# Small fp32 products on the two halves of TensorE in turn, in a four-layer hybrid network

## What is computed

```python
oa = gated_delta_rule(qa, ka, va, g.transpose(0, 2, 1), beta.transpose(0, 2, 1))
ob = moba_attention(split_heads(qb), split_heads(kb), split_heads(vb))
hc = mlstm_chunkwise(split_heads(qc), split_heads(kc), split_heads(v_c), i_pre, logf)
return jnp.concatenate([oa, ob, hc], axis=-1) @ w_out
```

```python
diff = bt[:, :, :, None, :] - bt[:, :, None, :, :]
dec = jnp.where(mask, jnp.exp(jnp.where(mask, diff, 0.0)), 0.0)
attn = jnp.einsum('bhtk,bhtsk->bhts', qt, dec * kt[:, :, None, :, :])
o_intra = jnp.einsum('bhts,bhsv->bhtv', attn, vt)
state = jnp.exp(b_last[:, :, 0, :])[..., None] * state + jnp.einsum(
    'bhsk,bhsv->bhkv', kt * jnp.exp(b_last - bt), vt)
```

## Time and profile before

| | |
|---|---|
| median of 3 runs | 2211.3 us (2209.76 to 2214.19) |
| the profiled execution | 2211.54 us |
| its span, first to last instruction | 2209.6 us |
| mean granted TensorE clock | 0.965 of full speed |
| busy: PE, PEld, DVE, ACT, POOL | 2058.1, 1914.5, 1644.6, 1082.2, 322.7 us |
| weight stream on the SP queue (q1) | 384.85 MB, 46.5% of 16 DMA engines' span |

### The profile page before, as it was taken

How to read it: one execution, slowest core, us unless ns; L and a number is a source line. 1 busy time by engine, 2 the same in 40 slices (tenths; PEclk the granted TensorE clock), 3 DMA queues, 4 the chain that set the end, 5 groups by cost and what they waited for, 6 DMA issues and landing times.

```text
span 2209.6 us, 35479 instructions
## 1 busy us (share of the span) xinstructions
PE 2058.1 (93%) x14804; PEld 1914.5 (87%) x14804; DVE 1644.6 (74%) x2175; ACT 1082.2 (49%) x1540; POOL 322.7 (15%) x269
## 2 busy tenths in 40 slices
PE   7999899999998999899989997898899988989998
PEld 7999789978987998799969986897799778968986
DVE  6698788566987578787575668986788588757884
ACT  4543473445434443553444434655565365646652
POOL 0200023010020002303010023520000136000020
PEclk9999999999999999899989998999999989999999
DMA  9888552134976578442225662332354532324442
GB/s 376 327 345 320 202 203 96 45 128 163 350 290 245 210 269 312 152 163 77 96 100 200 241 242 106 135 131 99 134 189 176 208 128 107 141 105 153 175 180 103
DMA packets 60079, 409.97 MB, mean 186 GB/s; under 512 B 6864, under 2 KB 6864, under 8 KB 13456
## 3 DMA queue, kind: packets, MB, share of 16 engines
q1 hardware_dynamic: 53712, 384.85, 46.5%
q0 software_dynamic: 5920, 22.43, 3.0%
q10 hardware_dynamic: 288, 0.42, 0.1%
HBM read 404.53 MB, written 3.15 MB: 185 GB/s over the span
## 4 chain that ended last, share of the span: by engine, by line
PE 74%; DVE 16%; ACT 4%; issue 2%; POOL 2%; DMA 1%; SPq 0%; POOLq 0%; DVEq 0%; ACTq 0%
PE ps L696 14%; PE ps L697 13%; PE ps L698 13%; PE ps L724 6%; PE ps L726 6%; PE ps L725 6%; DVE l L592 4%; PE ps L1755 2%; PE ps L709 2%; PE ps L710 2%; PE ps L711 2%; ACT h L577 1%; PE ps L1737 1%; PE ps L1632 1%; DMA w<-in_stream 1%
## 5 line engine op out<-in xcount | busy, mean ns | idle before, releaser
L696 PE MATMUL ps<-xh,h 128*128 128x256 f32 x2688 | 774.8, 288 | 30.7 <-DVE xl L913 8.7
L592 DVE TENSOR_TENSOR l<-w,h 128x2048 fp32r<-128x2048 f32 (+1 forms) x295 | 684.2, 2324 | 138.4 <-ACT h L577 137.9
L697 PE MATMUL ps<-xl,h 128*128 128x256 f32 x2688 | 762.6, 284 | 0.0
L698 PE MATMUL ps<-xh,l 128*128 128x256 f32 x2688 | 761.9, 283 | 0.0
L577 ACT CAST h<-w 128x2048 fp32r<-128x2048 f32 (+1 forms) x295 | 556.8, 1894 | 317.8 <-PE ps L726 145.3
L696 PEld LDWEIGHTS ps<-xh,h 128*128 128x128 f32 x2688 | 517.8, 193 | 43.8 <-issue 25.2
L697 PEld LDWEIGHTS ps<-xl,h 128*128 128x128 f32 x2688 | 517.7, 193 | 1.5 <-issue 1.4
L698 PEld LDWEIGHTS ps<-xh,l 128*128 128x128 f32 x2688 | 517.3, 192 | 0.0
L724 PE MATMUL ps<-h,hh 128*128 128x512 f32 x528 | 209.7, 397 | 9.0 <-DVE l L592 9.0
L726 PE MATMUL ps<-h,hl 128*128 128x512 f32 x528 | 207.5, 393 | 0.0
L725 PE MATMUL ps<-l,hh 128*128 128x512 f32 x528 | 207.3, 393 | 0.0
(11 more groups left out here) (413 smaller groups left out, 3030.0 us busy)
## 6 DMA issues: line engine op xcount, KB each, us to landing
w<-in_stream SPq DMA_DIRECT2D x361, 1024.0 KB, 4.9
GB<-in_vec POOLq DMA_DIRECT2D x20, 512.0 KB, 6.1
w<-in_stream SPq DMA_DIRECT2D x8, 512.0 KB, 4.1
gate<-in_vec POOLq DMA_DIRECT2D x6, 512.0 KB, 3.9
cst<-in_cst POOLq DMA_DIRECT2D x1, 1160.0 KB, 9.0
memf<-in_memT SPq DMA_DIRECT2D x2, 512.0 KB, 5.4
xf<-in_xT POOLq DMA_DIRECT2D x1, 1024.0 KB, 8.7
kv<-mk POOLq DMA_DIRECT2D x2, 512.0 KB, 6.3
```

Source lines behind the costliest of these rows:

```text
L592: e.tensor_tensor(k.L[m % NH][:, 0:z], k.W[n % NW][:, 0:z], k.H[m % NH][:, 0:z], SUB).then_inc(k.lo_done, 1)
L696: p.matmul(P[:, 0:T], H[:, r, o], xh[:, r, :], start=r == 0, stop=False)
L697: p.matmul(P[:, 0:T], H[:, r, o], xl[:, r, :], start=False, stop=False)
L698: i = p.matmul(P[:, 0:T], L[:, r, o], xh[:, r, :], start=False, stop=r == 7)
```

## The change

Every small product that uses half of the array's rows or gives half of its outputs is issued in turn with one of the other half. For that gdn's matrices of levels 0 to 5 are kept as their two diagonal blocks of 64x64, one in partitions 0 to 63 and one in 64 to 127 (`small`, 12 units of 64 columns), six units to a bank; a level has then two groups where it had four, on PE, DVE, ACT and POOL. The off-diagonal block goes to `AO`, and the inverse is written at last to the full `XF`, whose left half POOL clears once. The numbering of units changes (`unit`, `block`), so that a group for one half of the rows is followed by one for the other. `RB` is kept in partitions 64 to 127 too. hgrn's `A` holds only blocks of 64x64, one bank a level in turn instead of two. The constants shrink from 2320 to 1616 columns.

```diff
+def pe_halves(p, P, sem, left, right):
+
+    for j in range(6):
+        for r in (LO, HI):
+            x = p.matmul(P[r, j * 64:j * 64 + 64], left(r, j), right(r, j), start=True, stop=True)
+            if j == 5:
+                x.then_inc(sem, 1)
...
-    for lv in range(1, 7):
-        for g in range(4):
+    for lv in range(1, 6):
+        for g in range(2):
             b = GBANK[f"U{lv}", g]
             P = take(k, p, b)
...
+            pe_halves(p, P, s, lambda r, j: k.Al[r, 6 * g + j, :], lambda r, j: k.Xb[r, 6 * g + j, :])
             k.freed[b] = ga(l, f"U{lv}", g)
...
+                l_, r_ = (k.Ub, k.XT) if x else (k.XT, k.Ub)
+                pe_halves(p, P, s, lambda r, j: l_[r, 6 * g + j, :], lambda r, j: r_[r, 6 * g + j, :])
```

Decays and scores, by halves of the rows, into two banks:

```diff
+        for j in range(3):
+            for i, r in enumerate((LO, HI)):
+                g = 2 * n + i
+                h, a = unit(3 * g + j) if n < 2 else (OFF[3 * i + j], 1)
+                c = 64 * i + 32 * q + h
+                row = k.ident[r, c:c + 1].to_broadcast([64, 128])
+                x = p.matmul(P[i][:, j * 128:j * 128 + 128], row, k.RB[r, a * 128:a * 128 + 128], start=True, stop=True)
...
+            x = p.matmul(P[i][:, j * 128:j * 128 + 128], lT[r, pr, s * 128:s * 128 + 128], rT[r, pr, t * 128:t * 128 + 128], start=True, stop=True)
```

DVE, ACT and POOL in gdn:

```diff
-    v.tensor_copy(k.RB[Q0, :], G[Q0, ALL]).then_inc(s, 1)
+    for q in (Q0, Q2):
+        v.tensor_copy(k.RB[q, :], G[Q0, ALL]).then_inc(s, 1)
...
+        if g < 4:
+            v.tensor_tensor(k.AT[LO, u, :], P[LO, :, 0:64], k.Dk[LO, u, 0:64], MUL).then_inc(s, 1)
+            v.tensor_tensor(k.AT[HI, u, :], P[HI, :, 64:128], k.Dk[HI, u, 64:128], MUL).then_inc(s, 1)
+            v.tensor_tensor(k.AO[LO, u, :], P[LO, :, 64:128], k.Dk[LO, u, 64:128], MUL).then_inc(s, 1)
...
+            v.tensor_tensor(k.Xb[:, u, :], k.Xb[:, u, :], P, SUB).then_inc(s, 1)
...
+                e.copy(k.Ub[:, u, :], P).then_inc(s, 1)
...
+            g_.tensor_tensor(k.Al[:, 6 * g:6 * g + 6, :], k.AT[:, 6 * g:6 * g + 6, :], m, MUL).then_inc(k.gg.sem, 1)
```

hgrn's levels, states and sums:

```diff
+    P = take(k, p, 4 + n % 2)
+    for j in range(8):
+        for o, r in enumerate((LO, HI)):
+            c = slice(j % 2 * 128 + o * 64, j % 2 * 128 + o * 64 + 64)
+            i = p.matmul(P[r, j * 64:j * 64 + 64], Kl[:, j // 2, c], Ql[:, j // 2, c], start=True, stop=True)
...
+        for h in range(4):
+            c = slice(h * 128, h * 128 + 128)
+            for d in range(2):
+                n = i if d == 0 else 3 - i
+                a, r = n // 2, HI if n % 2 else LO
+                x = p.matmul(P[d][:, c], k.kt[r, d, a, c], k.hv[r, a, c], start=True, stop=True)
...
+            for r in (LO, HI):
+                p.matmul(P[r, c], k.A[r, 2 * h + a, :], k.hv[r, a, c], start=h == 0, stop=False, skip_group_check=True)
...
+    mb = mask.bitcast(I32).unsqueeze(1).to_broadcast([128, 8, 64])
+    v.wait_ge(*k.hp(l, name, 1))
+    v.copy_predicated(k.A[:, :, :], mb, rr(k.ps[4 + n % 2][:, :], "p (u t) -> p u t", u=8)).then_inc(k.hv_.sem, 1)
```

More of the change, by code:

```diff
@@ L1328, in mixer1_buffers @@
     assert f["end"] <= z, (f["end"], z)
-    big, off, row, half = [128, 12, 128], [128, 6, 128], [128, T + 1], [128, 2, 384]
-    k.Xb, k.Al, k.AT, k.XT, k.Dk = (k.place(n, big, z + 6144 * i) for i, n in enumerate(("Xb", "Al", "AT", "XT", "Dk")))
+    big, small, off, row, half = [128, 12, 128], [128, 12, 64], [128, 6, 128], [128, T + 1], [128, 2, 384]
+    k.Xb, k.Al = k.place("Xb", small, z), k.place("Al", small, z + 3072)
+    k.XF = k.place("XF", big, z + 6144)
+    k.AT, k.AO = k.place("AT", small, z + 12288), k.place("AO", small, z + 15360)
+    k.XT, k.Ub = k.place("XT", small, z + 18432), k.place("Ub", small, z + 21504)
+    k.Dk = k.place("Dk", big, z + 24576)
     k.ATo, k.Do = k.place("ATo", off, z + 30720), k.place("Do", off, z + 33792)
-    k.Ub = k.place("Ub", big, gq)
     r = k.stack(z, A=row, B=row, y=row, e=row, gl=row, G=row, M=row, ir=row)
@@ L1757, in pe_gdn @@
-                k.freed[b] = gv(l, f"V{lv}", n * g + x)
-            if g % 2:
-                yield
+                l_, r_ = (k.Ub, k.XT) if x else (k.XT, k.Ub)
+                pe_halves(p, P, s, lambda r, j: l_[r, 6 * g + j, :], lambda r, j: r_[r, 6 * g + j, :])
+                k.freed[b] = gv(l, f"V{lv}", 2 * g + x if lv < 5 else 3 * g + 2 * x)
+            yield
+    for g in range(2):
+        b = GBANK["U6", g]
+        P = take(k, p, b)
+        p.wait_ge(*gv(l, "V5", 3 * g))
+        for j in range(6):
+            i = p.matmul(P[HI, j * 64:j * 64 + 64], k.AO[LO, 6 * g + j, :], k.Xb[LO, 6 * g + j, :], start=True, stop=True)
+        i.then_inc(s, 1)
+        k.freed[b] = ga(l, "U6", g)
+        yield
@@ L1760, in pe_gdn @@
+    for g in range(2):
+        b = GBANK["V6", g]
+        P = take(k, p, b)
+        p.wait_ge(*ga(l, "U6", g))
+        p.wait_ge(*gv(l, "V5", 3 * g + 2))
+        for j in range(6):
+            i = p.matmul(P[LO, j * 64:j * 64 + 64], k.Ub[HI, 6 * g + j, :], k.XF[HI, 6 * g + j, 64:128], start=True, stop=True)
+        i.then_inc(s, 1)
+        k.freed[b] = gv(l, "V6", g)
+        yield
     p.wait_ge(k.m1_silu, 5 * l + 5)
@@ L1927, in act_gdn @@
     for lv in range(1, 7):
-        for g in range(4):
-            e.wait_ge(*gp(l, f"U{lv}", g))
-            if lv == 1 and g == 0:
-                e.wait_ge(*gp(l, "Q2", 1))
+        for g in range(2):
+            u = slice(6 * g, 6 * g + 6)
+            P = rr(bank(f"U{lv}", g)[:, 0:384], "p (u t) -> p u t", u=6)
             if lv < 6:
-                e.copy(flat3(k.Ub, g), bank(f"U{lv}", g)[:, 0:384]).then_inc(s, 1)
-            else:
-                e.copy(k.Ub[HI, 3 * g:3 * g + 3, 0:64], rr(bank("U6", g)[HI, 0:192], "p (u t) -> p u t", u=3)).then_inc(s, 1)
-            if g % 2:
-                yield
+                e.wait_ge(*gp(l, f"U{lv}", 2 * g + 1))
+                e.copy(k.Ub[:, u, :], P).then_inc(s, 1)
+            else:
+                e.wait_ge(*gp(l, "U6", g))
+                e.copy(k.Ub[HI, u, :], P[HI, :, :]).then_inc(s, 1)
+            yield
         yield
@@ L2094, in pe_mlstm @@
     s, q, kk = mp.sem, k.cq[:, 0:3, :], k.cq[:, 3:6, :]
-    yield from pe_decays(k, p, l, 1, lambda g: 6 + g % 2, mp, mv_, ma, k.rv(l, "RB", 1))
+    yield from pe_decays(k, p, l, 1, lambda g: 6 + g % 2, mp, mv_, ma, k.rv(l, "RB", 3))
     p.wait_ge(k.m1_silu, 5 * l + 4)
-    for g in range(6):
-        P = take(k, p, 6 + g % 2)
-        pe_units(k, p, kk, q, g, P).then_inc(s, 1)
-        k.freed[6 + g % 2] = mv_(l, "P", g)
-        if g % 2:
-            yield
+    for n in range(3):
+        pe_units(k, p, kk, q, n, [take(k, p, 6 + i) for i in range(2)], s)
+        for i in range(2):
+            k.freed[6 + i] = mv_(l, "P", 2 * n + i)
+        yield
     p.wait_ge(*k.m1_out(l, "c16", 1))
@@ L2375, in mixer2_steps @@
             before = [] if n == 0 else ["mD"] if n == 1 else [f"m{n - 2}"]
-            k.hv_.add(l, **{x: 2 for x in before}, **{f"k{n}0": 2, f"k{n}1": 2})
+            k.hv_.add(l, **{x: 1 for x in before}, **{f"k{n}0": 2, f"k{n}1": 2})
             k.hp.add(l, **{"mD" if n == 0 else f"m{n - 1}": 2})
@@ L2757, in scores @@
         p.wait_ge(*da(l, "T", 3))
-        for c in range(2):
-            b, r = (6, 2)[c], slice(64 * c, 64 * c + 64)
-            P = take(k, p, b)
-            for a in range(2):
-                x = p.matmul(P[:, a * 256:a * 256 + 256], k.qT[r, h, a * 128:a * 128 + 128], k.qT[r, 4 + h, :], start=True, stop=True)
-            x.then_inc(s, 1)
-            k.freed[b] = da(l, f"e{h}", 2 * c + 1)
+        P = [take(k, p, b) for b in (6, 2)]
+        for a in range(2):
+            for c, r in enumerate((LO, HI)):
+                x = p.matmul(P[c][:, a * 256:a * 256 + 256], k.qT[r, h, a * 128:a * 128 + 128], k.qT[r, 4 + h, :], start=True, stop=True)
+                if a:
+                    x.then_inc(s, 1)
+                    k.freed[(6, 2)[c]] = da(l, f"e{h}", 2 * c + 1)
     def turn(h):
```

319 lines of the change are left out of this document (145 added, 174 removed).

## The result

| | before | after |
| --- | --- | --- |
| median of the runs, us | 2212.7 (2209.8 to 2219.7, 4 runs) | 2182.5 (2177.7 to 2185.4, 4 runs) |
| ratio, 95% interval | | 0.9859 (0.9837 to 0.9880) |
| span of the profiled execution, us | 2209.6 | 2180.0 |
| mean granted clock of TensorE | 0.965 | 0.957 |

The account below looks back on a forecast made before the run. PE alone was taken to bound the first mixer's levels, DVE parts of both mixers. Savings of 19.8 us (first mixer) and 5.4 us (second) a layer, doubled to 50.4, gave 2161 us; range 2142 to 2186.

Parts of the forecast that it names:

- Levels: First mixer, 369 to 441 us: half products side by side save 53.4 ns on each of 312 records, 16.7 us a layer.
- Decays and scores: First mixer, array halves in turn: mlstm's decays save 2.0 us and its scores 1.8 us a layer; gdn's counted at nothing.
- Mlstm's scores: First mixer: three runs of score products with array halves in turn, one seam already overlapping; 1.8 us a layer saved.
- DVE's term: First mixer, where DVE sets the time, 331 to 369 us: net 1.8 us less; 1.3 us a layer with RB's copies.
- the copies into RB: First mixer, near 296 us: two further DVE copies on the chain, 0.29 and 0.42 us, of which 0.5 counts.
- Heads and changes of shape: First mixer after 369 us: 0.10 us per tile-shape change, two changes in each of four runs, 0.8 us given back.
- The chain inside a level: First mixer, levels 2 to 5: less PE work covers casts ahead of ACT's copies; 1.2 us a layer given back.
- rival B: Levels become a chain of waits, copy behind cast or subtraction behind weight split: 6.8 us a layer, 2174 us; 15%.
- The second mixer: Halved copies into A save 2.6 us, states 1.8, sums over states 1.0: together 5.4 us a layer.
- the states: Second mixer, 1470 to 1500 us, PE bare: three runs of 16 records save 0.6 us each, 1.8 us a layer.
- The sums: Second mixer, sums over states, 1470 to 1500 us: two runs of 24 records save 0.5 us each, 1.0 us a layer.
- The clock: DVE-bound stretches with PE idle for a fifth could run partly at 1.2 GHz: a microsecond or two each.

## Why the prediction was right, and where it was not

**Levels: right in size.** 53.4 ns a record was forecast for 312 records, 16.7 us. A level fell from 8.0 to 4.2 us as worked out, and level 1's first half, counted as covered by DVE, gave its part too: 19.2 us of products in five levels of a layer. The 1.2 us that the sum left out (some 62 ns of sequencer time per matmul where hardware decode is off, by the Trainium skill, "TensorE: Matmul & The Clock Gate", section "Wait — 56ns, not 53.3ns?") are not there: 12 half products, 24 records, take 0.70 us, 58 ns each. Nor does what the Trainium skill says in "TensorEngine Tiling (Array Packing)", section "Gotcha 1: PSUM Pressure", that different row tiles cannot use one bank at the same time, bind here: the two halves write different partitions of one bank in these same 0.70 us.

**Decays and scores: right.** Runs of 12 records fell from 1.60 to 0.94 us, 0.66 each, against 0.67 forecast. Mlstm's scores gave 1.5 where 1.8 stood.

**DVE's term: right.** A's scores to level 1: 1.9 us less, forecast 1.8 of that part. The stretch from the stage's start to the scores got 0.9 longer where the sum had 0.5 for the copies into RB. Together 1.0 of the 1.3.

**Heads and changes of shape: too small.** "0.8 us" a layer stood for two changes in each of four runs. Without its idle time the piece from level 1 to the last level fell by 18.4 us, of which 21.2 were products, so 2.8 us are given back. In the timeline each entry into a 64x64 run costs about 0.1 us, and so does each way out; every level's pair of U groups pays as well, 0.12 us (1.47 us for 48 records and 0.75 for the next 24, for 1.40 and 0.70), which the sum did not have.

**The chain inside a level: too small, and not the chain that was meant.** The sum took 1.2 us a layer, "near the low end"; it is 4.3 and 5.1 us of new idle time. None of it waits for ACT's copy of Ub behind a cast, the first case of rival B; its other case, a subtraction behind a weight split, came in one place of a layer, 1.3 us at level 6, and not 2 us in each of four levels. Of 5.5 us in layer 1, and all but one of them in layer 0: 1.05 <-DVE cq, 0.78 and 1.08 <-DVE gate (a bank), 0.51 <-ACT mo, 0.55 and 0.75 <-DVE Xb behind a weight split, and 0.78 "issue". Work of other streams and a bank shared with another stage, which a slower PE never met.

**The second mixer: wrong.** "They hold 8.0% of the chain from 1404 to 1470, 5.3 us, so 2.6 us go" is the step that failed. The share of a chain says what waited last, not how far behind the next one is. The next was ACT's copy of dqk, behind exponentials that POOL feeds: behind the 3.1 us for A at the third meet PE already stood 0.8 us a layer for it in the kernel before (the 1.6 us in its row above), so nothing saved ahead of it could show. Of the products, the states gave 0.4 us a layer where 1.8 stood: 1.7 us of work went, but with turns both queues' first states end together, and the second products now wait 1.26 us for ACT's two copies of ST, which one queue's products had covered before. The sums gave 1.0 as forecast. The third meet came 4.0 us sooner after the first than before (9.8 for 13.7 us), and the fourth then 6.9 us later after the third (15.5 for 8.6): what was saved went into the wait of 6.14 us and the half clock behind it. With ACT's copies in another place the second mixer's change gives 6.6 us in the stages of both layers (12.6 in the medians, some 5 either way). So what failed was above all the claim that it would show in this order; by the traces a part of its worth was too large as well, 2.8 us of it in the states.

**The clock: missing from the sum.** "For a microsecond or two each" stood in the range only. The mean granted clock fell from 0.965 over 2209.6 us to 0.957 over 2180.0: by that, 155 us at 1.2 GHz before and 187 after. Counted in the records, PE was busy in 119 us of the first and 137 of the second, and loses at most half of the difference, 9 us, where it is the bound. One piece of it is seen plainly: 26 records in 5.0 us after the wait in the second mixer (window 1398 to 1403, above), while the kernel before did 53 in the 6 us from 1424. Another stands at the end of layer 1's levels, where 6.8 us at 1.2 GHz (from 1047.8) are most of why that layer gives 12.8 us and not 16.9, and one at 61 us, before anything that the change touches, behind which most of the +2.1 of the table's first row appears. Why the clock falls at one execution's 61 us and not at another's is open.

So of the 20.8 us between forecast and span, 9.9 lie in the first mixer (new waits 7.0 beyond the 2.4 counted, shape changes 4.0, half clock about 3, small terms about 1, less 5.0 us of products that were counted as covered), 9.1 in the second, and most of the rest ahead of both. That the time still lies in the range is in part luck: the upper end was drawn for waits inside the levels (rival B), and nearly half of what used it up was the second mixer, for which the range had no term of that size.

## What to carry to other kernels

When PE's work shrinks, read for each queue not what PE waits for now but what stands second: a copy that is ready and sits in an in-order queue behind work that waits for a third engine, or a bank that another stream frees. Where two waits end close together at one place, removing one can be worth next to nothing and removing both a good deal (1.8 us, nothing, and 6.2 here), so a change that "does nothing" there should be tried again with the other one moved. And where medians of five runs and the length of a stage in the traces disagree, look at the same stage in every kernel that has it unchanged: here both stages of the second mixer together repeat within 2 us, while executions of one kernel lie up to 10 us apart. Small products should be turned from one side of the array to the other product by product, not group by group; by groups less than half of what PE gains in a level is left (8.0 to 6.2 us, not to 4.2).
